# Gate products inside two scans, conditioning loaded in pieces

## The reference

```
sh1, sc1, g1, sh2, sc2, g2 = split(silu(c) @ w_ada[l] + b_ada[l], 6)      # conditioning; the same for c_ctx
h   = rmsnorm(x) * (1 + sc1) + sh1
z   = h @ w_in                                     # q, k, v, mLSTM inputs, conv inputs, three gates
y_da, y_ml, y_cv = diff_attention(z), bidirectional_mlstm(z), short_conv(z)
m   = sigmoid(gate_da) * (y_da @ w_da) + sigmoid(gate_ml) * (y_ml @ w_ml) + sigmoid(gate_cv) * (y_cv @ w_cv)
x   = x + g1 * (m @ w_o)
h2  = rmsnorm(x) * (1 + sc2) + sh2
x   = x + g2 * peer(h2)                            # top-16 experts of 16384 for each of 8 heads
```

## Time and profile before

| what | value |
|---|---|
| median of 3 runs | 5519.85 us (5511.01 to 5521.69) |
| the profiled execution, its own time | 5514.17 us |
| its span in the trace | 5512.4 us |
| PE / DVE / ACT / POOL busy, share of the span | 73% / 50% / 31% / 27% |
| mean share of full TensorE clock granted | 0.846 |
| norm1 to route of segment a, with the start | 0 to 701.9 us |
| ml_back and merge of segment d | 3579.0 to 3855.4 us |

### The profile page before, as it was taken

How to read it: one execution, slowest core, us unless ns; L and a number is a source line. 1 busy time by engine, 2 the same in 40 slices (tenths; PEclk the granted TensorE clock), 3 DMA queues, 4 the chain that set the end, 5 groups by cost and what they waited for, 6 DMA issues and landing times.

```text
span 5512.4 us, 62725 instructions
## 1 busy us (share of the span) xinstructions
PE 4011.6 (73%) x21784; PEld 2394.3 (43%) x21784; DVE 2774.3 (50%) x6649; ACT 1716.9 (31%) x4747; POOL 1474.6 (27%) x1295
## 2 busy tenths in 40 slices
PE   3889678889887787667566677778567797655555
PEld 1668554556564454324232234667334565311111
DVE  1321747654448545765455443431685445844454
ACT  0210137342443442343322222210235253422222
POOL 0000012222223233333344441000232222345453
PEclk7889889989999898888788888779888899877776
DMA  6344458768899899989999996214896899999998
GB/s 264 138 154 166 164 210 289 266 235 312 296 362 358 337 408 395 398 362 383 373 420 410 398 420 236 69 54 165 349 392 226 312 393 381 351 382 421 402 421 356
DMA packets 259311, 1712.61 MB, mean 311 GB/s; under 512 B 37713, under 2 KB 39345, under 8 KB 71601
## 3 DMA queue, kind: packets, MB, share of 16 engines
q0 software_dynamic: 184320, 1342.26, 61.0%
q1 hardware_dynamic: 74672, 366.33, 18.0%
HBM read 1690.46 MB, written 17.92 MB: 310 GB/s over the span
## 4 chain that ended last, share of the span: by engine, by line
PE 40%; DMA 24%; DVE 16%; ACT 6%; issue 4%; POOL 3%; DVEq 2%; ACTq 2%; PEld 1%; SPq 1%; PEldq 0%; POOLq 0%
PE psum L445 25%; DMA arena<-in_uv,arena 20%; PE psum L802 9%; DVE arena L2053 6%; POOL arena L1137 3%; DMA arena<-in_w_ada 1%; PEld psum L445 1%; DVE arena L1968 1%; PE psum L405 1%; DVE arena L1961 1%; DVE arena L1962 1%; PE psum L626 1%; PE psum L627 1%; ACT arena L1232 1%; DMA arena<-in_w_mix 1%
## 5 line engine op out<-in xcount | busy, mean ns | idle before, releaser
L1137 POOL DMA_INDIRECT arena<-in_uv,arena x1280 | 1470.7, 1149 | 4003.8 <-PE psum L802 2638.2
L802 PE MATMUL psum<-arena 64*64 64x512 f32 x10240 | 1546.1, 732 | 881.3 <-ACTq L1484 802.7
L2053 DVE CUSTOM_DVE_ANT_0 arena<-arena 128x1024 f32<-128x1024 f32 x1280 | 1547.7, 1225 | 1146.4 <-DMA arena<-in_uv,arena 1087.5
L445 PE MATMUL psum<-arena 128*128 128x256 f32 (+2 forms) x8480 | 1954.0, 388 | 98.6 <-DVEq L1503 67.6
L445 PEld LDWEIGHTS psum<-arena 128*128 128x128 f32 (+1 forms) x8480 | 1615.1, 195 | 541.3 <-issue 183.0
L802 PEld LDWEIGHTS psum<-arena 64*64 64x64 f32 x10240 | 386.0, 155 | 1811.6 <-ACTq L1484 1135.5
L1477 ACT ACTIVATE arena<-arena 128x2 f32<-128x2 f32 x640 | 130.8, 204 | 1550.0 <-DVEq L2055 1536.3
L1483 ACT ACTIVATE arena<-arena 128x64 f32<-128x64 f32 x1280 | 375.9, 340 | 46.1 <-issue 2.1
L405 PE MATMUL psum<-arena 128*128 128x128 f32 (+1 forms) x680 | 124.2, 335 | 293.9 <-DVE arena L1562 99.4
L1480 ACT ACTIVATE arena<-arena 128x1 f32<-128x1 f32 x1280 | 307.9, 287 | 45.1 <-issue 0.7
L1920 DVE TENSOR_TENSOR arena<-arena,psum 128x256 f32<-128x256 f32 x120 | 50.5, 421 | 466.8 <-ACT arena L1387 465.1
(11 more groups left out here) (202 smaller groups left out, 2365.9 us busy)
## 6 DMA issues: line engine op xcount, KB each, us to landing
arena<-in_w_in SPq DMA_DIRECT2D x92, 1024.0 KB, 6.8
arena<-in_w_mix SPq DMA_DIRECT2D x120, 768.0 KB, 6.9
arena<-in_w_ada SPq DMA_DIRECT2D x32, 1536.0 KB, 16.3
arena<-in_w_wq SPq DMA_DIRECT2D x40, 1152.0 KB, 9.3
arena<-in_w_wo SPq DMA_DIRECT2D x20, 1024.0 KB, 6.7
arena<-in_uv,arena POOLq DMA_INDIRECT x1280, 11.1
arena<-ada_rows SPq DMA_DIRECT2D x15, 512.0 KB, 5.8
arena<-x_rows SPq DMA_DIRECT2D x14, 512.0 KB, 7.1
```

Of the source, the lines that this page charges most:

```text
L445: ins = mm(out, a, b, start=(i == 0), stop=(i == last))
L802: ins = mm(psum[o, r_ * 512:r_ * 512 + 512], DIAG[rows, c, :], RING[rows, sl, D + half * 512:D + (half + 1) * 512], start=first, stop=last ...
L1137: pool.indirect_dma_start(RING[:, sl, :], None, io["uv"], bass.IndirectOffsetOnAxis(IDX[:, t, h * TOPK + k:h * TOPK + k + 1], 0)).then_inc ...
L2053: V_.tensor_tensor_reduce(out=RING[:, sl, 0:D], in0=RING[:, sl, 0:D], in1=XT[:, u % 2, :], scale=1.0, scalar=0.0, op0=ALU.mult, op1=ALU.ad ...
```

## The change

Gate products: for the scans `("ml", 0, (0,))` and `("ml_back", 1, (1, 2))` the 24 gate chains of the merge that follows are computed in the scan, as 12 chunks of two gate blocks each. In every scan unit one chunk comes between `ahead` and the products, and the rest behind `turned`: two in the context scan (4 units), one in ml_back (6 units). They use PSUM banks 0 and 1, and ACT takes their sigmoid to SBUF. The merge of these two keeps the 24 branch chains, in 8 chunks, and its ACT work in the mix goes.

Conditioning: two quarters come before the first norm is applied, inside norm1, where the context tokens are loaded ahead of them. The barrier before norm1 goes. The other six run at the ends of qkv, mlp and mc, after da, at block 4 of the merge's mix, and behind its w_o products. Their loads are issued in pieces between weight chunks, except that of `ada(3)`. The store to DRAM is split in four.

```diff
+AHEAD = {("ml", 0, (0,)): 0, ("ml_back", 1, (1, 2)): 1}
+GATE_CHUNKS = 3 * KD // 2
+def gate_chunks(kind, l, pairs, i, late):
+    if (kind, l, pairs) not in AHEAD:
+        return range(0)
+    units = len(ml_units(kind, l, pairs))
+    per = GATE_CHUNKS // units
+    return range(per * i + 1, per * i + per) if late else range(per * i, per * i + 1)
...
@@ PE
+            def gates_ahead(kind, l, pairs, i, late):
+                for n in gate_chunks(kind, l, pairs, i, late):
+                    p, b = AHEAD[kind, l, pairs], n % 2
+                    ht = buf(l, p, "HT", [KD, PW])
+                    w = view(weights(l, "gate", n), [2, KD, P])
+                    if fills[b]:
+                        pe.wait_ge(bank_out[b], fills[b])
+                    for j in range(2):
+                        ins = chain(bank(b)[:, j * PW:(j + 1) * PW], [(w[:, j, k, :], ht[:, k, :]) for k in range(KD)])
...
             def norm1(kind, l, pairs):
-                if l == 0 and pairs == (0,):
-                    ada1(0)
...
+                if (l, pairs) == FIRST:
+                    pe.wait_ge(s("csilu"), 1)
+                    ada(0)
+                    ada(1)
                 barrier()
...
@@ ml
                     if i + 1 < len(units):
                         ahead(i + 1)
+                    gates_ahead(kind, l, pairs, i, False)
...
                     if i + 1 < len(units):
                         turned(i + 1)
+                    gates_ahead(kind, l, pairs, i, True)
                     yield
...
@@ merge
                 for c in range(KD):
+                    if c == ADA_AT and (l, pairs) == FIRST:
+                        ada(6)
                     for br in range(3):
+                        if (l, p) in AHEAD_OF:
+                            if br == 0:
+                                w = view(weights(l, "branch", c), [3, CH, P])
+                            (b,) = fill(("mix", l, p, c, br))
+                            full(chain(bank(b)[:, PW:2 * PW], [(w[:, br, k, :], ys[br][:, k, :]) for k in range(CH)]))
...
@@ ACT, ml
                     if i + 1 < len(units):
                         ahead(i + 1)
+                    for when in (False, True):
+                        for n in gate_chunks(kind, l, pairs, i, when):
+                            p = AHEAD[kind, l, pairs]
+                            (b,) = whole(("ahead", l, p, n))
+                            empty(A.activation(gated(l, p, n), bank(b).rearrange("p (a b) -> p a b", a=2), ACT.Sigmoid), b)
...
@@ SP, merge
-                        chunks(1)
+                        if br == 0 or (l, p) not in AHEAD_OF:
+                            chunks(1)
+                        if br == 0 and (l, pairs) == FIRST and c < 3:
+                            ada_load(6, ((0, 1), (2,), (3,))[c])
+                        if br == 0 and (l, pairs) == FIRST and c > ADA_AT:
+                            ada_load(7, (c - ADA_AT - 1,))
```

More of the change, by code:

```diff
@@ L109, in steps @@
     return [8.0]
+FIRST, ADA_AT = (0, (0,)), 4
 FIRST_ROUTES = ((1, (1,)),)
@@ L190, in chunk_list @@
                 out += [(l, "in", CHUNK_NAMES.index((name, hh))) for hh, name in EDGE_OPS]
+            elif (kind, l, pairs) in AHEAD:
+                out += [(l, "gate", i) for i in range(GATE_CHUNKS)]
             elif kind == "merge":
-                out += [(l, "mix", i) for i in range(24)] + [(l, "wo", c) for c in range(4)]
+                out += [(l, "branch", c) for c in range(KD)] if (l, pairs[0]) in AHEAD_OF else [(l, "mix", i) for i in range(24)]
+                out += [(l, "wo", c) for c in range(4)]
             elif kind == "route":
@@ L198 @@
 CHUNKS = chunk_list()
-CHUNK_WIDTH = dict(gates=KD * 16, mix=1536, wo=2048, wq=2304)
+CHUNK_WIDTH = dict(gates=KD * 16, mix=1536, gate=2048, branch=1536, wo=2048, wq=2304)
 CHUNK_WIDTH["in"] = 2048
@@ L857, in ada1_load @@
-            def ada1_load(q):
-                sp.wait_ge(s("ada_mm"), AQ + q)
-                for g in range(4):
[L860 to L865, removed]
+            xs = buf(0, 0, "XS", [2, D])
+            for t in tiles_of(0):
+                sp.dma_start(xs[:, t, :], io["ctx"][0, t * P:(t + 1) * P, :]).then_inc(s("xs_in"), 16)
@@ L885, in load_chunk @@
                 width = CHUNK_WIDTH[name]
[L886 to L887 removed]
+                dst = view(W_AT + (n % WSLOTS) * WSLOT, [width])
+                if name == "gate":
+                    src, dst = io["w_mix"][l, 2 * i:2 * i + 2, :, 0:KD * P].rearrange("a p n -> p a n"), dst.rearrange("p (a n) -> p a n", a=2)
+                elif name == "branch":
+                    src, dst = io["w_mix"][l, 3 * i:3 * i + 3, :, KD * P:].rearrange("a p n -> p a n"), dst.rearrange("p (a n) -> p a n", a=3)
+                else:
+                    src = io["w_gates"][l] if name == "gates" else io["w_" + name][l, i]
+                sp.dma_start(dst, src).then_inc(w_in[n % WSLOTS], 16)
                 state["w"] += 1
@@ L971, in ml @@
             def ml(kind, l, pairs):
-                if (l, pairs) == first:
-                    ada1_load(2)
-                for u in ml_units(kind, l, pairs):
+                for i, u in enumerate(ml_units(kind, l, pairs)):
+                    chunks(sum(len(gate_chunks(kind, l, pairs, i, late)) for late in (False, True)))
                     yield
```

191 lines of the change are left out of this document (114 added, 77 removed).

## The result

| | before | after |
|---|---|---|
| median (lowest to highest) of 4 runs each | 5520.77 us (5511.01 to 5522.03) | 5435.82 us (5431.24 to 5442.60) |
| ratio, 95% interval | | 0.985 [0.9838, 0.9862] |
| the profiled execution | 5514.17 us | 5442.60 us |

The account below looks back on a forecast made before the run. TensorE, busy 73% of the span, was taken as the bound, with idle and half-speed time to recover. The terms summed to -82.6 us: 5514.2 became 5431.6, plus 5.7 for the median, forecast 5437; range 5420 to 5466 at 0.8.

Parts of the forecast that it names:

- Start: Start to norm1's end: two quarters first, no wait for store and later quarters, 67.5 instead of 131.0 us, -63.5.
- Quarters at stage ends: qkv, mlp, mc: each quarter costs TensorE 5.34 and VectorE 2.26 us, less cover: +7.2, +6.8, +5.4.
- the cover that I credited: mlp: 1.0 us of TensorE idle time before the scan covers part of the quarter, leaving about +6.8.
- Scans: Context scan and ml_back: gate matmuls fill pauses and raise the clock; 166 us of gates cost 117, +66.0 and +51.1.
- The return of the clock: Scans: the clock rises about 5 us into the first gate chunk, which costs 2.4 us.
- two covers that I named: Scans: a 6.9 us late chunk covers the 2.5 us to `within`'s end; an early one covers 3.1 us of `arguments`, load, exp.
- rival of scans at half clock: Scans: gates run at half speed, 332 us instead of 166, kernel slower at 5654 us; chance 0.04.
- scans that don't fill: Scans: gate chunks only push pauses back, each scan grows by the whole 83.1 us, kernel 5488; chance 0.07.
- Table loads: Scans: 14 more loads of 1.28 us cost 0; rival, they hold the scan's chain, 18 us, 5455; chance 0.07.
- The rival's reason: Scans, table-load rival: the load is issued only when the exp's input is ready; 18 us, chance 0.07.
- Transfers late: Rival: w_ada pieces delay weight chunks, 10 us in qkv, mlp, mc and 8 at the merge's quarter, 5455; chance 0.11.
- the merge's wait: Merge of segment a: the quarter at the fourth block waits 3.6 us for its loads, bounds 0 and 12.

Follow-up runs that it names:

- unused matmuls: Kernel with the conditioning alone, plus 8 and 12 chains of matmuls with unread results in its two scans: 5494.7 us, 0.996 of before.
- all chunks late: Changed kernel with all gate chunks of a scan unit behind `turned`, none before the products: 5434.04 us, 0.9853 of before.
- quarters early: Changed kernel with the quarters in qkv, mlp and mc one matmul step before the stage's end: 5425.68 us, 0.984 of before.
- both early: Changed kernel with both gate chunks of each ml_back unit before the products, none behind `turned`: 5460.02 us, 0.9901 of before.
- the kernel without table loads: Changed kernel with exp in place of the sigmoid on the scans' gate products: 5437.88 us, 0.986 of before.

## Why the prediction was right

| term | predicted | profiled executions |
|---|---|---|
| start to the end of norm1 | -63.5 | -66.1 |
| quarter in qkv, in mlp, in mc | +7.2, +6.8, +5.4 | +8.1, +8.4, +5.5 |
| context scan, ml_back | +66.0, +51.1 | +63.6, +52.5 |
| merge of segment a, of segment d | -72.1, -83.5 | -73.5, -83.8 |
| sum | -82.6 | -85.3 |

**Start.** The mechanism was right. The 2.6 us are in the step from the sums to the columns: I took 9.0 and 0.5, and it was 6.7 from the last sum (52.1) to the columns (58.8). Only half the rows are stored now, which may be why; no run tests it. The three weight chunks cost nothing that shows.

**Quarters at stage ends.** In mc the full price, less the 1.7 us that the clock gave back, came out. In qkv 0.8 of the 8.1 is the clock at the stage's start, which I hadn't counted: its first 128 records took 30.8 us, 30.0 before. In mlp the cover that I credited did come, but the clock was low where the quarter stands (0.62 from 213.1 to 217.0 us), so that it took 7.04 us instead of 5.34:

```profile
213.13 7.04 PE L502 MATMUL psum<-arena 128*2 128x384 f32 x64
```

With matmuls left behind the quarter, 1.1 to 1.7 us came back in each of the three stages. Some small sums of mine are off by 0.1 to 0.3 us and decide nothing: 7.6 less a tail of 1.0 is 6.6, not 6.8, and three state waits at 1.25 and 0.66 are 5.7, not 5.4.

**Scans.** The scan's own work had the price that I gave it: 3.3 us for `ahead`, 1.9 for 16 product records. The waits for the state remained, at 0.88, 0.88 and 1.25 in the context scan and at 1.25 in ml_back, and no other was left. The return of the clock cost 2.3 in the context scan, where I had 2.4. That scan came out 2.4 short mainly because its opening took 14.5 us instead of 15.8: the quarter ahead of it took the half-clock stretch, and its first pairs ran in 0.49 us. In ml_back the return cost only 1.1, but the clock fell again in two units, which cost 3.4. I hadn't thought of that, and the two sizes partly cancel.

Of the two covers that I named, the runs support the late chunk (without it +22 us), and show that the early one isn't needed. For the late one I had named only the wait, 8 us of the 22, and nothing of the clock behind it (10.6) or of the stage's end (3.3). The rival of scans at half clock, and that of scans that don't fill, are refuted by the windows after and by the unused matmuls.

**Table loads** at 0: shown, by taking them away. The rival's reason, that a load is issued only when the exp's input is ready, held before the change but not after: the load runs while ScalarE waits for that input. I had argued this from the early chunk that stands over the exp. That reason is too narrow: with all chunks late the sigmoids and their loads are still there, no chunk stands before the products, and the scans keep their length.

**Transfers late.** This rival was partly right, in one place. I had 3.6 for the merge's wait; it was 4.35 and 0.86 for a chunk. In qkv, mlp and mc no such wait decided anything: with the quarters early, TensorE idles 0.5 to 1.3 us there. Moving one load removes both waits.

**The sum** was made on the profiled execution, and there the terms give -85.3, but the two profiled executions differ by 71.6. The other 14 lie in stages whose code is unchanged, and the medians don't show them: 5520.77 less 5435.82 is 85.0. This execution of before was 6.6 us under its median, and that of after 6.8 above. So the stage terms, each within 2.6 us, are what the prediction earned. That the median came within 2 us of 5437 is in part luck, as single executions of either kernel lie 11 us apart.

## What to carry to other kernels

Look for the stage in which a chain of small steps holds TensorE at half clock, and move matmuls there that depend on nothing in it: 166 us of them cost 116 here. Place them where they cover the longest pause, not only where they fit. Two short pauses close together, in four units, cost 8 us in waiting and 11 more in clock. A load that is hidden in a long stage may show when the change shortens that stage, so price each load against the stage's new length.

## What was unexpected of the hardware

Short pauses cost clock. With 1.25 us of pause, 0.66 of work and 1.99 more of pause, the clock went to half for 6.8 to 10 us, in all four units of both early. The pause of 1.25, with no other in the unit, was enough in some units. In the change's ml_back two of four units behind such a pause have a stretch of some 3.5 us at half, about 10 us after it, and in the other two the clock stayed:

```profile
3562.25 0.66 PE L430 MATMUL psum<-arena 128*128 128x128 f32 x4 [1.25 <-DVEq L1887]
...
3573.22 8.56 PE L485 MATMUL psum<-arena 128*128 128x256 f32 x32
...
3619.94 7.10 PE L485 MATMUL psum<-arena 128*128 128x256 f32 x32
```

In five other kernels with this stage unchanged it was one unit of the four. What decides which unit it hits isn't known.

Stages with the same code took one of a few lengths some 3 us apart. The qkv stage of layer 0's latent tokens, in the change and then in the kernel without table loads, two kernels with the same code for it:

```profile
684.10:803.10 119.00, 117.74 (x640) 83.70 (x640) 51.69 (x104) 30.29 (x102) 29.89 (x29) 0.98 0.83 299
```

```profile
682.30:798.00 115.70, 115.56 (x640) 82.32 (x640) 51.60 (x104) 30.25 (x102) 28.59 (x28) 1.00 0.84 305
```

In ten other executions, that of before among them, it was 115.7 to 116.1. Layer 0's latent scan came out at 115.3, 118.4 or 121.3. This scan is 3.1 of the 14 us above (115.3 before, 118.4 after); the rest is spread over many stages, whose lengths differ by up to 3.3 us, some longer and some shorter. So a change of a few us is to be read from its own stages.
